# A two-block transformer kernel: 42 instead of 32 tokens leave the dense expert products, a gathered row is one operation, and so is a value piece's remainder

## The reference

```
q = (xn @ w_pq).reshape(B, S, 8, 2, 128)
s1, s2 = scores of q's halves against 128 keys each
v1, i1 = lax.top_k(s1, 16);  v2, i2 = lax.top_k(s2, 16)
vs, ci = lax.top_k(v1[..., :, None] + v2[..., None, :], 16)   # of 256 pairs
eidx = i1[ci // 16] * 128 + i2[ci % 16];  gates = softmax(vs)
act = gelu(einsum('tkd,td->tk', expert_u[eidx], xn))          # k: 8 heads x 16
out = einsum('tk,tkd->td', act * gates, expert_v[eidx])
```

## Time and profile before

| | us |
|---|---|
| median of 3 runs (2958.08 to 2959.38) | 2959.25 |
| profiled execution | 2959.44 |
| its span, first to last instruction | 2957.7 |
| PE busy | 2910.0 |
| DVE busy | 1969.9 |
| ACT busy | 1388.9 |
| POOL busy | 593.0 |

### The profile page before, as it was taken

One profiled execution on the slowest core, in us unless ns is written; L12 is line 12 of the kernel. 1 busy time (PEld: TensorE's weight loads), 2 busy tenths in 40 slices (PEclk: granted clock), 3 DMA queues, 4 the chain that ended last, 5 costly groups with the idle time before them and its releaser, 6 DMA issues.

```text
span 2957.7 us, 41749 instructions
## 1 busy us (share of the span) xinstructions
PE 2910.0 (98%) x16599; PEld 2625.5 (89%) x16599; DVE 1969.9 (67%) x2753; ACT 1388.9 (47%) x1992; POOL 593.0 (20%) x555
## 2 busy tenths in 40 slices
PE   8999999999999999999999999999999999999999
PEld 7998778888888887978789999999999999999999
DVE  5556654444444445464568999677787888888876
ACT  4355544444444444354444444444455555555553
POOL 2000000000000000150004888488710000000000
PEclk9999999999999999999999999999999999999999
DMA  8554356666665554544567888899997888888764
GB/s 292 162 168 151 115 175 222 224 234 231 226 197 183 187 198 140 176 153 156 177 218 252 226 224 224 279 328 336 343 375 266 314 324 323 324 316 316 260 215 141
DMA packets 244456, 692.88 MB, mean 234 GB/s; under 512 B 46569, under 2 KB 98825, under 8 KB 210880
## 3 DMA queue, kind: packets, MB, share of 16 engines
q1 hardware_dynamic: 194560, 600.81, 59.4%
q0 software_dynamic: 47168, 86.54, 10.5%
q10 hardware_dynamic: 2560, 3.21, 0.4%
HBM read 654.70 MB, written 33.69 MB: 233 GB/s over the span
## 4 chain that ended last, share of the span: by engine, by line
PE 49%; DVE 2%; ACT 0%; issue 0%; ACTq 0%; DVEq 0%
PE banks L2231 16%; PE banks L2286 15%; PE banks L2232 8%; PE banks L2287 7%; PE banks L2307 1%; PE banks L2309 1%; PE banks L2308 1%; DVE weights_lo L195 1%; PE banks L2250 0%; DVE peer_features L376 0%; DVE top_index L2049 0%; ACT weights_hi L188 0%; PE banks L2259 0%; PE banks L2275 0%; DVE row_gates L2063 0%
## 5 line engine op out<-in xcount | busy, mean ns | idle before, releaser
L195 DVE TENSOR_TENSOR weights_lo<-weights,weights_hi 128x1024 fp32r<-128x1024 f32 (+4 forms) x1080 | 1228.4, 1179 | 702.8 <-ACT weights_hi L188 700.7
L188 ACT ACTIVATE weights_hi<-weights 128x1024 fp32r<-128x1024 f32 (+4 forms) x1080 | 1046.5, 1017 | 1370.6 <-PE banks L417 639.7
L2231 PE MATMUL banks<-peer_features,weights_hi 128*128 128x448 f32 (+1 forms) x2304 | 734.8, 378 | 6.1 <-DVE weights_lo L195 6.1
L415 PE MATMUL banks<-weights_hi,features_hi 128*128 128x512 f32 (+3 forms) x1600 | 608.0, 380 | 26.2 <-DVE weights_lo L195 23.0
L2232 PE MATMUL banks<-peer_features,weights_lo 128*128 128x224 f32 (+1 forms) x2304 | 610.2, 265 | 0.0
L417 PE MATMUL banks<-weights_hi,features_lo 128*128 128x512 f32 (+3 forms) x1600 | 602.5, 377 | 0.0
L416 PE MATMUL banks<-weights_lo,features_hi 128*128 128x512 f32 (+3 forms) x1600 | 602.4, 377 | 0.0
L2286 PE MATMUL banks<-peer_features,weights_hi 128*128 128x448 f32 x1568 | 492.5, 374 | 0.0
L2231 PEld LDWEIGHTS banks<-peer_features,weights_hi 128*128 128x128 f32 x2304 | 432.0, 187 | 48.6 <-DVE weights_lo L195 8.7
L2232 PEld LDWEIGHTS banks<-peer_features,weights_lo 128*128 128x128 f32 x2304 | 439.2, 191 | 0.0
L2197 POOL DMA_INDIRECT expert_gates<-peer_choice x224 | 399.4, 1783 | 182.3 <-DVEq L2071 102.8
(11 more groups left out here) (400 smaller groups left out, 2729.3 us busy)
## 6 DMA issues: line engine op xcount, KB each, us to landing
weights<-in_expert_u SPq DMA_DIRECT2D x128, 1024.0 KB, 6.3
weights<-in_expert_v SPq DMA_DIRECT2D x128, 1024.0 KB, 6.4
weights<-in_w_ffn_gate SPq DMA_DIRECT2D x44, 1024.0 KB, 5.2
weights<-in_w_ffn_up SPq DMA_DIRECT2D x44, 1024.0 KB, 5.2
weights<-in_w_ffn_down SPq DMA_DIRECT2D x44, 1024.0 KB, 4.8
weights<-in_w_in SPq DMA_DIRECT2D x48, 900.0 KB, 5.0
weights<-in_w_out SPq DMA_DIRECT2D x32, 1024.0 KB, 5.1
weights<-in_w_in SPq DMA_DIRECT2D x24, 704.0 KB, 4.2
```

The source lines that it names most:

```text
L188: act.activation(hi[:, k, n], raw[:, k, n], ACT.Copy).then_inc(self.hi_ready, 1 + skip)
L195: last = dve.tensor_tensor(lo[:, k, n], raw[:, k, n], hi[:, k, n].bitcast(F32), ALU.subtract)
L415: pe.matmul(out, xh, wh, start=first, stop=False)
L2231: pe.matmul(self.bank(n % 3, 2 * cols), wh[:, k, :], F[:, k, :, 0:cols], start=(k == 0), stop=False)
```

## The change

`ROWS` goes to 42 and `DENSE` to 214. The gathered tokens lie in three groups of 42 on 126 partitions, so 43 gathers are needed for each table instead of 32. Their dots and additions take a whole row of 2048 at once: 31 dots at steps 76 to 139, twelve more at V0-1 to V0+21, then 43 additions at V0+27 to V0+115. The lists of rows and gates are no longer copied group by group on DVE; DVE turns them once and ACT moves them by six transfers at step 70, so POOL's first gather comes behind 116 scatters. The ten additional tokens still scatter their gates, into cells behind the table. From V0 on, the remainder of a piece is one operation, which waits for both halves (`split_lo_whole`).

```diff
+    def split_lo_whole(self, dve, stream, i, j, half):
+
+        hi, lo, raw = self.piece(self.hi, half, stream), self.piece(self.lo, half, stream), self.raw(j, half, stream)
+        dve.wait_ge(self.hi_ready, i * 16 + (2 * (2 * (self.fills + j) + half) + 2))
+        dve.tensor_tensor(lo, raw, hi.bitcast(F32), ALU.subtract).then_inc(self.lo_ready, 1)
...
-    WQ, ROWS, ZEROED = 384, 32, 8
+    WQ, ROWS, ZEROED = 384, 42, 8
...
-        SUM = [*range(78, 142)]
-        DOTS = SUM[-1] + 1
-        free = [s for s in range(V0 + 17, V0 + 118) if (s - V0) % 16 not in (0, 5, 6, 8, 10, 14)]
-        ADD = [free[k * len(free) // (2 * ROWS)] for k in range(2 * ROWS)]
+        GROUPS = P // ROWS
+        RUNS, USED = -(-SLOTS // GROUPS), GROUPS * ROWS
+        MINE = slice(P - ROWS, P)
+        SUM = [76 + c * 21 // 10 for c in range(31)] + [V0 - 1 + 2 * c for c in range(12)]
+        DOTS = SUM[-1] + 2
+        free = [s for s in range(V0 + 27, V0 + 118) if (s - V0) % 16 not in (0, 5, 6, 8, 10, 14)]
+        ADD = [free[k * len(free) // RUNS] for k in range(RUNS)]
...
+            lists = [rows[:, 1, 256 * n:256 * n + GROUPS * RUNS] for n in range(4)]
+            picked, picked_turned = lists[0].bitcast(U32), lists[1].bitcast(U32)
...
                     if t == ROW_TILE:
-                        for quarter in range(4):
-                            row_gate_part = row_gate[quarter * ROWS:quarter * ROWS + ROWS, 0, part * 8:part * 8 + 8]
-                            k = part * HP * TOPK + quarter * 8
-                            last = dve.tensor_copy(row_gate_part, gates_of[P - ROWS:P, t, k:k + 8])
-                        ch(last)
+                        ch(dve.tensor_copy(lists[2][:, part * HP * TOPK:(part + 1) * HP * TOPK],
+                                           gates_of[:, t, part * HP * TOPK:(part + 1) * HP * TOPK]))
+                        if part == PARTS - 1:
+                            turned = lambda x: x.rearrange("p (q c) -> p c q", q=GROUPS)
+                            full = SLOTS // GROUPS * GROUPS
+                            for of, to in ((picked, picked_turned), (lists[2], lists[3])):
+                                dve.tensor_copy(turned(to)[:, 0:SLOTS // GROUPS, :],
+                                                of[:, 0:full].rearrange("p (c q) -> p c q", q=GROUPS))
+                                last = dve.tensor_copy(turned(to)[:, SLOTS // GROUPS, 0:SLOTS - full], of[:, full:SLOTS])
+                            ch(last)
+                            dve.sem_inc(listed, 1)
...
+                                last = dve.tensor_copy(both[P - 32:P, :, 4 * quarter:4 * quarter + 4],
+                                                       both[32 * quarter:32 * quarter + 32, :, FULL:TOPK])
...
+                    if t == ROW_TILE:
+                        own = vif[:, 0:2, :].rearrange("p h k -> p (h k)")
+                        ch(dve.scalar_tensor_tensor(out=own, in0=iof[:, slots], scalar=past[:, 1:2], in1=own, op0=ALU.mult, op1=ALU.add))
...
+                        ch(dve.scalar_tensor_tensor(out=picked[:, slots], in0=eg[:, 0, slots], scalar=float(NKEYS), in1=eg[:, 1, slots],
+                                                    op0=ALU.mult, op1=ALU.add))
...
-                        if c % 8 == 0 and c < ROWS:
-                            pool.wait_ge(listed, c // 8 + 1)
+                        if c == 0:
+                            pool.wait_ge(moved, 16 * 2 * GROUPS)
...
+                        pool.indirect_dma_start(out=rows[0:USED, c % BUFS, :], out_offset=None, in_=rows_d if c < RUNS else values_d,
+                                                in_offset=bass.IndirectOffsetOnAxis(ap=pick[0:USED, c % RUNS:c % RUNS + 1], axis=0))\
...
-                    early, mixed = 124, 4
-                    for n, cell in enumerate(cells[:early]):
+                    early, mixed = 116, 4
+                    for cell in cells[:early]:
                         scatter(*cell)
-                        if n < BUFS:
-                            gather(n)
-                    for c in range(BUFS, 2 * ROWS):
+                    for c in range(BUFS):
+                        gather(c)
+                    for c in range(BUFS, 2 * RUNS):
...
+                        if s == RET + 60:
+                            act.wait_ge(listed, 1)
+                            for q in range(GROUPS):
+                                mine, to = slice(q * RUNS, (q + 1) * RUNS), slice(q * ROWS, (q + 1) * ROWS)
+                                act.dma_start(pick[to, :], picked_turned[MINE, mine]).then_inc(moved, 16)
+                                act.dma_start(row_gate[to, 0, :], lists[3][MINE, mine]).then_inc(moved, 16)
...
-                        ring.split_lo(dve, tiles, i, j, half)
+                        if s < V0:
+                            ring.split_lo(dve, tiles, i, j, half)
+                        else:
+                            ring.split_lo_whole(dve, tiles, i, j, half)
...
-                        for k in [k for k, at_step in enumerate(SUM) if at_step == s]:
-                            c, part = divmod(k, 2)
-                            if part == 0:
-                                dve.wait_ge(gathered[c % BUFS], 16 * (c // BUFS + 1))
-                            row, x_row = [y[:, part * D // 2:(part + 1) * D // 2] for y in (rows[:, c % BUFS, :], xg)]
-                            dve.tensor_tensor_reduce(row, row, x_row, 1.0, 0.0, ALU.mult, ALU.add, dots[:, part, c:c + 1])\
-                                .then_inc(row_summed, 1)
-                        for k in [k for k, at_step in enumerate(ADD) if at_step == s]:
-                            c, part = divmod(k, 2)
-                            if part == 0:
-                                dve.wait_ge(gathered[(ROWS + c) % BUFS], 16 * ((ROWS + c) // BUFS + 1))
-                            row, to = [y[:, part * D // 2:(part + 1) * D // 2] for y in (rows[:, (ROWS + c) % BUFS, :], row_sum)]
-                            weight = row_gate[:, 0, c:c + 1]
-                            if c > 0 or part > 0:
-                                dve.wait_ge(row_summed, 2 * ROWS + max(k - 1, 0))
+                        for c in [c for c, at_step in enumerate(SUM) if at_step == s]:
+                            dve.wait_ge(gathered[c % BUFS], 16 * (c // BUFS + 1))
+                            row = rows[0:USED, c % BUFS, :]
+                            dve.tensor_tensor_reduce(row, row, xg[0:USED, :], 1.0, 0.0, ALU.mult, ALU.add, dots[:, 0, c:c + 1])\
+                                .then_inc(row_summed, 2)
+                        for c in [c for c, at_step in enumerate(ADD) if at_step == s]:
+                            dve.wait_ge(gathered[(RUNS + c) % BUFS], 16 * ((RUNS + c) // BUFS + 1))
+                            row, weight, to = rows[0:USED, (RUNS + c) % BUFS, :], row_gate[:, 0, c:c + 1], row_sum[0:USED, :]
+                            dve.wait_ge(row_summed, 2 * (RUNS + c))
                             if c == 0:
                                 last = dve.tensor_scalar(to, row, weight, None, ALU.mult)
                             else:
-                                last = dve.scalar_tensor_tensor(out=to, in0=row, scalar=weight, in1=to, op0=ALU.mult, op1=ALU.add)
-                            last.then_inc(row_summed, 1)
+                                last = dve.scalar_tensor_tensor(out=to, in0=row, scalar=weight, in1=to,
+                                                                op0=ALU.mult, op1=ALU.add)
+                            last.then_inc(row_summed, 2)
...
-        self.g_rows = nc.dram_tensor("expert_gates", (P * NKEYS * dense, 1), F32, kind="Internal").ap()
-        self.g_d = self.g_rows.rearrange("(p e t) o -> p e (t o)", e=NKEYS, t=dense)
+        self.g_rows = nc.dram_tensor("expert_gates", (P * NKEYS * dense + P * SLOTS, 1), F32, kind="Internal").ap()
+        self.g_d = self.g_rows[0:P * NKEYS * dense, :].rearrange("(p e t) o -> p e (t o)", e=NKEYS, t=dense)
```

More of the change, by code:

```diff
@@ L2175, in _ @@
                     self.pool_chain.on(pool)(pool.iota(token_i[:, :], pattern=[[P, NT]], base=0, channel_multiplier=1))
-                    self.pool_chain.on(pool)(pool.tensor_copy(token[:, :], token_i[:, :]))
+                    ch = self.pool_chain.on(pool)
+                    pool.memset(by_key[:, 0, :], float(DENSE))
+                    pool.memset(by_key[:, 1, :], float(NKEYS * DENSE))
+                    pool.memset(past[:, 0:1], float(P * NKEYS * DENSE - (NT - 1) * P))
+                    pool.memset(past[:, 1:2], float(P))
+                    ch(pool.tensor_copy(token[:, :], token_i[:, :]))
+                    for n in range(2):
+                        step = by_key[:, n, ROW_TILE:ROW_TILE + 1]
+                        pool.affine_select(out=step, in_=step, pattern=[[0, 1]], compare_op=ALU.is_ge, fill=0.0,
+                                           base=P - ROWS - 1, channel_multiplier=-1)
```

(8 more changed lines are left out.)

47 lines of the change are left out of this document (20 added, 27 removed).

## The result

The changed kernel took 3102.03 us (median of 4 runs, 3099.17 to 3111.68) beside 2959.22 for the kernel before: ratio 1.0489 with a 95% interval of 1.0466 to 1.0512, 143 us slower. The forecast was 2955.5, and its range ended at 2966.

The account below looks back on a forecast made before the run. TensorE (PE) was taken to set the pace in both tables. From 2959.4 us, columns took 34.1 off, whole-remainder stalls added 25.3, the border 0.7 and score loads 4.2: 2955.5 us, range 2938 to 2966.

Parts of the forecast that it names:

- At nothing: Effects priced at zero: first-table remainder and dots, POOL's round, gather landings, last scatters, choice of experts, ACT's list transfers.
- rival 3: Score loads in the value steps land 3 us late or more and PE waits: 2971 to 2985 us, 15%.
- The columns: Matmul pairs in both tables: wide matmul 20 columns narrower, 8.33 ns less for each of 4096 pairs, 34.1 us less.
- the floor under the narrow matmul: Narrow matmuls in both tables: a minimum time of about 110 ns, so ten fewer columns there gain nothing.
- The whole remainder's hand-over: Value steps: one operation waits for both rounded halves, so DVE's spare time before PE's load shrinks from 1.15 to 0.13 us.
- Its sum: Value steps: PE stalls from whole remainders beside DVE's whole rows and other work, 25.3 us more in all.
- the evacuations: 14 value steps whose first chunk is evacuated behind the whole remainder: 6.2 us, plus 0.8 for the steps behind.
- the walk: Step-by-step carry through 118 value steps: DVE work over 2.67 us delays the next remainder, 0.13 us is free, the rest stops PE.
- The border: PE's first value step waits for a bank that DVE empties behind the remainder of V0+1: 0.7 us more.
- Late score loads: Value steps: DVE's scaling waits 1.4 us for scores in each of seven tight loads, 4.2 us more in the sum.
- Of the rivals, 2: Value steps: DVE's real room is larger, so few heavy steps overflow, 7 to 15 us back: about 2938 us, 20%.
- Rivals 1 and 4: Matmul pairs: the narrow matmul shrinks too, 2946.5 us, 10%; or pairs stay at 313 ns, 2979 us, 5%.

Follow-up runs that it names:

- e1: The changed kernel with gathers of 128 rows instead of 126, the two spare partitions getting row 0: 2968.53 us, ratio 1.0033.
- e9: The changed kernel with 128-row gathers and four scatters behind each of the first three gathers, whole remainders kept: 2957.92 us, ratio 0.9995.
- e8: The changed kernel with 128-row gathers, value remainders in halves and four scatters behind each of the first three gathers: 2947.77 us, ratio 0.9962.
- e6: The changed kernel with 128-row gathers and 140 instead of 116 scatters ahead of the first gather, whole remainders kept: 2976.15 us, ratio 1.0056.
- e5: The changed kernel with 128-row gathers, value remainders in halves and 140 instead of 116 scatters ahead of the first gather: 2966.75 us, ratio 1.0030.
- e3: The changed kernel with 128-row gathers and value remainders in two halves again: 2960.68 us, ratio 1.0006.

## Why the prediction was wrong

**The step that failed** stands under "At nothing": "Gathers have three dots' time, some 28 us, for 13.3 at most". The 13.3 us was the longest landing of a 128-row gather, and I carried it over to 126 rows as if the change left a gather alone except for its number. The change had made its shape another. The landing became 13.5 us in the median and 38.9 at the longest, longer than three dots' time, and weight pieces and score loads beside it became late too: a piece of `expert_u` lands in 8.8 us in the median (6.3 before), one of `expert_v` in 10.9 (6.4). The range could not hold this, because rival 3, the only one about transfers, priced late score loads by 3 us at seven places, and took the rest of the traffic as it was. Its place was one of the right ones (59.6 us of waits at the scaling), its price, 7 x 2.9 us, a third of that. The omission is a general one: I had checked which operations were added and how long each computes, but not the shape of the transfer that the same number (`ROWS` = 42, times three groups) decides.

**A second step, smaller,** in the same paragraph: "they are out 0.5 us into step 132, about when SP wants them". "About" was 16.8 us of SP's wait and, in PE's time, about 10 us: e1 is 10.6 us above e9. I had compared the time of issue and not that of landing, and not followed what lies behind SP's wait, namely weight pieces.

With both corrected, e9 took 2957.92 us where the prediction said 2955.5, so its other steps can be held against the trace of e9. That the sum is so near is in part luck: the columns gave 5 us less than forecast and the first table began 5 us late, and the whole remainder's stalls, 8 us smaller, made up for most of it.

- *The columns*: forecast 34.1 us less, steps of 4.88. In the first table a step without a stall takes 4.907, 13.6 us less over 128 steps. In the values such steps are of two kinds: in e8 20 take 4.86 and 65 take 4.90, 4.892 on average, 15.5 us less; 29 us together. Within a step pairs start 306.7 ns apart in both tables, 313.3 before: 6.6 ns less against the forecast 8.3. That it is not 12.5 speaks for the floor under the narrow matmul. Why some value steps are 0.05 us shorter stays open.
- *The whole remainder's hand-over*: forecast 0.13 us of spare time, and 0.64 us of stall at V0+61. The timeline of e9 there:

```profile
2506.42 2.29 DVE L202 TENSOR_TENSOR weights_lo<-weights,weights_hi 128x2048 fp32r<-128x2048 f32 x1
2508.62 2.35 DVE L2566 SCALAR_TENSOR_TENSOR row_tokens<-expert_rows,row_gates,row_tokens 126x2048 f32<-126x2048 f32 x1
2510.88 0.60 DVE L2591 TENSOR_TENSOR peer_features<-normed,peer_features 128x428 fp32r<-128x428 f32 x1
2511.39 0.60 DVE L2599 TENSOR_TENSOR normed<-normed,peer_scratch 128x428 f32<-128x428 f32 x1
2511.91 2.28 DVE L202 TENSOR_TENSOR weights_lo<-weights,weights_hi 128x2048 fp32r<-128x2048 f32 x1
...
2514.25 0.19 PEld L2315 LDWEIGHTS banks<-peer_features,weights_hi 128*128 128x128 f32 x1 [0.60 <-DVE weights_lo L202]
```

The row takes 2.26 us until the next operation (forecast 2.27), the split 0.51 (0.52); the remainder is over at 2514.19 and the load comes at 2514.25, 0.06 later (0.05), after 0.60 us idle. The mechanism is as forecast.
- *Its sum*: forecast 25.3 us. Over the same steps the pitch of e9 exceeds 4.86, the shorter kind, by 17.6, and by some 16 if counted from the average 4.892: 9.6 for the 23 steps behind row, split and product (14.1 forecast), 2.5 for the two behind dot and scaling (3.2), 4.7 for the evacuations (7.0), 0.8 for the nine small ones (1.0). Where two heavy steps follow each other the stall is the forecast one, 0.63; behind a single one it is 0.3 to 0.45 instead of 0.5 to 0.64. So the walk took too little room for a lone step, by 0.2 us or so. (All that the value steps lose against 4.892 comes to 28 us, 5.1 before; the last two stalls, 1.7 us each, are in both.) Taken back to halves, the cost is 10.2 us (e9 over e8), 9.4 (e6 over e5) and 7.9 (e1 over e3). These are net costs, as the next point but one shows.
- *The border*: 0.78 us at V0, forecast 0.7.
- *Late score loads*: forecast 4.2 us. In e9 DVE waits 7.0 us for them (3.8 before), and PE loses about 5.9 at V0+37, +69, +85 and +86. In e8, whose steps are faster, DVE waits twice as long, and PE loses about 10 us at V0+37, +53, +69, +85, +86, +101 and +102. The rows of e8 and of e9:

```profile
DVE normed L2570 <- DMA normed<-expert_scores: 15.0, 5, 3.9
DVE normed L2573 <- DMA normed<-expert_scores: 7.0, 4, 3.4
```

So in e8 the halves give back more than 10 us at the hand-overs and lose some of it again at the scores. This is rival 3's mechanism, a third of its price in e9 and half in e8.
- *A late start, not forecast*: the first step of the first table begins 2.3 to 5.7 us later in the changed kernel and those made from it (1560.0 to 1563.4 us in seven traces) than in the kernel before (1557.7); in e9 it is 4.9. Of these, 4.0 stand already at the first step of the layer (1468.9 against 1464.9), and the traces part between 1000 and 1200 us, ahead of it. No experiment was made on it, and the cause stays open. With it the parts close: 4.9 - 13.9 in the first table + 7.7 in the values is -1.3, and the span of e9 is 1.5 us below that of before.

Of the rivals, 2 (the hand-over costs little, 2938) has a part of the truth, since stalls were 17.6 and not 25.3, but e8 with halves, without the late hand-over at all, only reaches 2947.8. Rivals 1 and 4 are out by the pitch: 306.7 ns, neither 301 nor 313. That POOL's round of 8.7 us stays hidden held, once the transfers were right: in e9 no dot waits for its rows.

## What to carry to other kernels

When a tiling number changes, read off the shape of every transfer that follows from it, its partitions above all, and give each a price of its own; a gather that brings 126 rows for 128 cost 2.5% of a kernel by itself (74 us), and two unused rows were the cure. A DMA share that stays at 1 says nothing of how much is moved: read it beside the GB/s. And a scheduling fault of 10 us is cured in the hole where the engine idles, not at the front of its queue: 24 scatters ahead of everything took one stall of 10 us away and brought one of 19, 12 in the hole took the 10 away and brought none.

## What was not expected of the hardware

- A 1 MB gather of 126 rows held up all traffic beside it: 8 KB packets of the weights in the first table took 435 ns instead of 378 (counted from the records of 1600 to 2200 us), and the core moved 280 GB/s instead of 346 at the same DMA share.
- 112 rows (16 engines by the count in flight) are slow too, with packets of 465 ns, and two gathers of 64 rows cost 91 us against one of 128, which is more than 126 rows do (79).
- 20 columns fewer in the wide matmul and 10 in the narrow one shorten the pair from 313.3 to 306.7 ns, in both tables. Yet among value steps without a stall 20 take 4.86 us and 65 take 4.90 (e8), where before none took less than 5.009.
